# Routed experts of a mixture-of-experts encoder layer: 66 blocks of one expert with the weights standing, against 46 rounds of packed experts with the tokens standing

## The reference

```python
idx = top 6 of 64 experts per token, out of the best 4 of 8 groups
w = scores[idx] / sum * 2.5
for each expert e, for its tokens xb:
    hb = silu(xb @ w_e_gate[e]) * (xb @ w_e_up[e])      # 1024 -> 256
    routed[token] += (hb @ w_e_down[e]) * gate          # 256 -> 1024
y = layer_norm(ALPHA * x + routed + shared expert)
```

## Time and profile before

| | |
|---|---|
| runs | 2017.0, 2020.99, 2020.8 us, median 2020.8 |
| profiled execution, its own time | 2016.74 us |
| its span, first to last instruction | 2014.9 us |
| busy: PE, PEld, DVE, ACT, POOL | 95%, 65%, 32%, 17%, 11% |
| first block's first product to last block's last | 1182.48 to 1973.24 us |
| moved by DMA over the span | 337.04 MB |

### The profile page before, as it was taken

How to read it: one execution, slowest core, us unless ns; L and a number is a source line. 1 busy time by engine, 2 the same in 40 slices (tenths; PEclk the granted TensorE clock), 3 DMA queues, 4 the chain that set the end, 5 groups by cost and what they waited for, 6 DMA issues and landing times.

```text
span 2014.9 us, 24123 instructions
## 1 busy us (share of the span) xinstructions
PE 1912.1 (95%) x9388; PEld 1304.8 (65%) x9388; DVE 639.3 (32%) x1060; ACT 343.4 (17%) x453; POOL 227.0 (11%) x310
## 2 busy tenths in 40 slices
PE   6999999999999999999999989999999999999991
PEld 3444466666666555655555468887788878887781
DVE  5011158888888720012257810000000000000005
ACT  1111121111111111110013012222222222222220
POOL 0000000000000000000000412222222222222220
PEclk9999999999999999999999989999999999999996
DMA  5115011111110011111700269999999999999984
GB/s 202 42 42 188 0 42 32 32 31 31 31 31 11 11 52 52 41 43 57 283 32 22 102 212 336 330 330 337 345 333 329 327 337 329 326 329 328 336 273 146
DMA packets 129230, 337.04 MB, mean 167 GB/s; under 512 B 11664, under 2 KB 68016, under 8 KB 112304
## 3 DMA queue, kind: packets, MB, share of 16 engines
q1 hardware_dynamic: 109904, 283.13, 37.8%
q0 software_dynamic: 19296, 53.50, 12.7%
HBM read 305.65 MB, written 47.71 MB: 175 GB/s over the span
## 4 chain that ended last, share of the span: by engine, by line
PE 86%; DVE 9%; ACT 2%; issue 1%; DMA 1%; DVEq 0%; POOLq 0%; SPq 0%; ACTq 0%; POOL 0%
PE pA L873 24%; PE pg L544 10%; PE pg L571 9%; PE pg L694 8%; PE pX L884 6%; PE pB L884 6%; PE pB L725 4%; PE pB L772 2%; PE pA L772 2%; PE pA L717 2%; PE pg L584 2%; PE pB L627 2%; PE pX L785 1%; PE pA L664 1%; PE pA L627 1%
## 5 line engine op out<-in xcount | busy, mean ns | idle before, releaser
L571 PE MATMUL pg<-rA,hw 128*128 128x384 f32 x768 | 259.6, 486 | 0.7 <-ACT aTr L948 0.7
L873 PEld LDWEIGHTS pA<-rA,ew 128*128 128x128 f32 x2112 | 243.5, 194 | 16.8 <-issue 15.3
L873 PEld LDWEIGHTS pA<-rB,rEF 128*128 128x128 f32 x2112 | 241.0, 192 | 15.8 <-issue 15.8
L873 PE MATMUL pA<-rA,ew 128*128 128x128 f32 x2112 | 243.8, 277 | 1.1 <-ACT rA L1049 1.1
L873 PE MATMUL pA<-rB,rEF 128*128 128x128 f32 x2112 | 241.1, 275 | 0.0
L544 PE MATMUL pg<-rEF,rA 128*128 128x512 f32 x448 | 195.3, 598 | 3.1 <-ACT rCD L927 3.1
L571 PEld LDWEIGHTS pg<-rA,hw 128*128 128x128 f32 x768 | 140.6, 190 | 84.1 <-ACT aTr L948 0.9
L694 PE MATMUL pg<-rA,hw 128*128 128x384 f32 x512 | 165.3, 486 | 0.0
L544 PEld LDWEIGHTS pg<-rEF,rA 128*128 128x128 f32 x448 | 85.8, 192 | 110.0 <-issue 110.0
L694 PEld LDWEIGHTS pg<-rA,hw 128*128 128x128 f32 x512 | 97.2, 190 | 67.6
L1484 DVE TENSOR_TENSOR rA<-rA,pA 128x256 f32<-128x256 f32 x33 | 13.9, 422 | 387.1 <-ACT rA L1055 387.1
(11 more groups left out here) (233 smaller groups left out, 2005.3 us busy)
## 6 DMA issues: line engine op xcount, KB each, us to landing
ew<-w_e_gate SPq DMA_DIRECT2D x33, 1024.0 KB
ew<-w_e_up SPq DMA_DIRECT2D x33, 1024.0 KB
ew<-w_e_down SPq DMA_DIRECT2D x33, 1024.0 KB, 9.1
rEF<-w_e_gate SPq DMA_DIRECT2D x33, 1024.0 KB
rEF<-w_e_up SPq DMA_DIRECT2D x33, 1024.0 KB
rEF<-w_e_down SPq DMA_DIRECT2D x33, 1024.0 KB, 10.2
hw<-w_in SPq DMA_DIRECT2D x40, 512.0 KB, 3.9
rEF<-w_in SPq DMA_DIRECT2D x5, 2048.0 KB, 9.1
```

The source lines that it names most:

```text
L571: last = mm(pg[:, n * 512:n * 512 + HALF], hw3[m][:, c, :], x1T[:, c, n * HALF:(n + 1) * HALF], start=(c == 0), stop=(c == KC - 1))
L873: last = mm(pA[:, o:o + P], w[:, c, j * P:(j + 1) * P], xT[n][:, c, :], start=(c == 0), stop=(c == KC - 1))
```

## The change

**Units and rounds.** An expert's tokens get units of 32 slots instead of blocks of 128. Experts are ranked by count; a rank has a fixed number of units (`rooms`: rank 0 one, ranks 1 to 10 four, ranks 11 to 42 three, ranks 43 to 63 two; 179 in all), and the ranks come in a fixed order (`ranks_in_turn`). Four units make a round of 128 slots, so there are 45 rounds, written out one by one. What does not fit (of the expert of rank 0, 124 tokens for this input) goes into a further block of 128 in a loop: 46 rounds.

**The tokens stand.** In a round PE's `up` puts the transposed tokens of one expert in 32, 64 or 128 columns of the array and moves that expert's gate and up weights, 512 columns, past them. `pieces(t)` lists these parts: one expert's slots from an even unit on make a piece of 64, a whole round of 128, and what is left over 32. Of the 45 rounds 3 have one piece (128), 18 have two (17 times 64 and 64, once 64 and 32), 20 have three (64, 32 and 32, in one order or the other) and 4 have four of 32: 115 pieces. For each of the 8 slices of the contraction the pieces come one after the other. The down products are cut likewise. The hidden values now come out with tokens as rows and are transposed (`hidden_turn`, 2 transposes).

**Weights.** Six buffers instead of two; each of the 64 experts is loaded once, and once more the one in the rest loop, 65 loads for 66. SP can start the first after the out projection.

**A row for each slot.** `y_dram` has 8 rows for each token; the k-th expert of a token writes row k. The scatter is a plain write of the filled slots alone and does not wait for the one before. At the end 6 rows a token are loaded (18.9 MB in 12 transfers instead of 3.1 MB in 6) and summed: four by PE (products with the identity), one pair by POOL, the rest by DVE. The shared expert's result stays in SBUF; its 7 stores are gone.

**Tables.** `slots` on DVE has 26 operations where it had 16 before the first one on all 2304 columns; two of them wait for short products on PE (`ranks`, `rooms_given`).

```diff
+KSTRIDE = 8
+UNIT = 32
+UNITS = P // UNIT
+def rooms():
+    return [1] + [4] * 10 + [3] * 32 + [2] * 21
+def ranks_in_turn():
+    large, middle, small = list(range(10, 0, -1)), list(range(11, 43)), list(range(63, 42, -1))
+    first, small = small[:4], small[4:]
+    mixed = sorted(((i + 0.5) / len(g), r) for g in (large, small, middle) for i, r in enumerate(g))
+    return first + [r for _, r in mixed] + [0]
...
+def pieces(t):
+    out = []
+    for j in range(E):
+        a = max(STARTS[j], t * UNITS) - t * UNITS
+        z = min(STARTS[j + 1], (t + 1) * UNITS) - t * UNITS
+        while a < z:
+            n = 4 if a == 0 and z == 4 else 2 if a % 2 == 0 and z - a >= 2 else 1
+            out.append((j, a * UNIT, n * UNIT))
+            a += n
+    return out
...
+        weights = (rA[:, :], ew[:, :], rEF[:, EW:], rCD[:, EW:], rCD[:, 0:EW], rB[:, :])
+        gate_up = [w[:, 0:4 * D] for w in weights]
+        wd = [slabs(w[:, 4 * D:6 * D], 2) for w in weights]
...
+            sp.wait_ge(of_filled, NT)
+            for j in range(NB):
+                if j == 1:
+                    sp.wait_ge(oh_ready, 1)
+                if j == 2:
+                    sp.wait_ge(sh_gu, NT)
+                if j == 4:
+                    sp.wait_ge(oh_used, NK)
+                if j == 5:
+                    sp.wait_ge(sh_acc, NT)
+                    sp.wait_ge(x2_stored, 16 * NT)
+                e = expert_in_turn(j)
+                load_gate_up(e, j)
+                load_down(e, j)
...
+            for t in range(NR):
+                for j in range(E - NB):
+                    if last_round(j) == t:
+                        sp.wait_ge(gu_filled, t + 1)
+                        load_gate_up(expert_in_turn(j + NB), j % NB)
+                for j in range(E - NB):
+                    if last_round(j) == t - 1:
+                        sp.wait_ge(y_filled, t)
+                        load_down(expert_in_turn(j + NB), j % NB)
...
+                sp.wait_ge(rest_free, r + 1)
+                load_gate_up(e, more)
+                load_down(e, more)
...
+            yb = d["y_dram"].rearrange("(t k) n -> t k n", k=KSTRIDE)
+            for i in range(NT):
+                if i == NB - 1:
+                    sp.wait_ge(sum_filled, 1)
+                    sp.wait_ge(half_added, 1)
+                    sp.wait_ge(yb_used, 1)
+                n = i % (NB - 1)
+                for m in range(2):
+                    three = slice(3 * m, 3 * m + 3)
+                    sp.dma_start(land[n][:, three, :], yb[i * P:(i + 1) * P, three, :]).then_inc(s_yb[n][m], 16)
...
-            def up(b, n, r):
-                pe.wait_ge(xt_ready, b + 1)
-                pe.wait_ge(s_wgu[n], r * 32 + 32)
-                for m, w in ((0, wg[n]), (1, wu[n])):
-                    for j in range(2):
-                        o = n * 512 + (2 * m + j) * P
-                        for c in range(KC):
-                            last = mm(pA[:, o:o + P], w[:, c, j * P:(j + 1) * P], xT[n][:, c, :],
-                                      start=(c == 0), stop=(c == KC - 1))
+            def up(t):
+                n = t % 2
+                pe.wait_ge(xt_ready, t + 1)
+                if t >= 2:
+                    pe.wait_ge(h_ready, t - 1)
+                for j, _, _ in pieces(t):
+                    pe.wait_ge(s_wgu[j % NB], 32 * (j // NB + 1))
+                for c in range(KC):
+                    for j, o, w in pieces(t):
+                        last = mm(gu[n][o:o + w, :], xT[n][:, c, o:o + w],
+                                  at(gate_up_home(j % NB)[0], gate_up_home(j % NB)[1] + c * F, [[2 * D, 2], [1, F]]),
+                                  start=(c == 0), stop=(c == KC - 1))
...
-                    for j in range(2):
-                        last = mm(pairY[n][:, m * 512:(m + 1) * 512], hT[n][:, j, :],
-                                  wd[n][:, j, m * 512:(m + 1) * 512], start=(j == 0), stop=(j == 1))
+                    for k in range(2):
+                        for j, o, w in pieces(t):
+                            last = mm(pB[o:o + w, m * 512:(m + 1) * 512], hT[n][:, k, o:o + w],
+                                      wd[j % NB][:, k, m * 512:(m + 1) * 512], start=(k == 0), stop=(k == 1))
...
+            gathered_turn(0)
+            gathered_turn(1)
+            for t in range(NR):
+                up(t)
+                if t >= 1:
+                    down(t - 1)
+                hidden_turn(t)
+                if t + 2 <= NR:
+                    gathered_turn(t + 2)
+            down(NR - 1)
...
+                for k in range(TOPK - 2):
+                    if k == 3:
+                        pe.wait_ge(s_yb[n][1], 16 * (i // (NB - 1) + 1))
+                    for m in range(2):
+                        last = mm(pairY[i % 2][:, m * 512:(m + 1) * 512], ident,
+                                  land[n][:, k, m * 512:(m + 1) * 512], start=(k == 0), stop=(k == TOPK - 3))
...
+                ve.wait_ge(half_added, i + 1)
+                v.tensor_tensor(acc[:, i, :], acc[:, i, :], land[i % (NB - 1)][:, TOPK - 2, :], ALU.add).then_inc(yb_used, 1)
+                ve.wait_ge(yb_used, i + 1)
+                ve.wait_ge(sum_filled, i + 1)
+                v.tensor_tensor(acc[:, i, :], acc[:, i, :], pairY[i % 2][:, :], ALU.add).then_inc(sum_taken, 1)
...
+            for t in range(4):
+                gather(t)
+            for t in range(NR):
+                if t >= 1:
+                    scatter(t - 1)
+                if t + 4 <= NR:
+                    gather(t + 4)
+            scatter(NR - 1)
...
+                g.tensor_tensor(land[n][:, TOPK - 2, :], land[n][:, TOPK - 2, :], land[n][:, TOPK - 1, :],
+                                ALU.add).then_inc(half_added, 1)
```

More of the change, by code:

```diff
@@ L228, in build @@
         gate, low, high = (scratch(NK, "hw") for _ in range(3))
-        nblk, incl, base = (scratch(E, "hw") for _ in range(3))
+        starts_rep, rooms_rep = scratch(P, "hw"), scratch(P, "hw")
+        keyrow, ahead, match, given, over = (work[:, n * E:(n + 1) * E] for n in range(5))
+        base, room = given, work[:, 5 * E:6 * E]
+        rest, resti_n, incl, shift = (work[:, n * E:(n + 1) * E] for n in range(6, 10))
+        keycol = second[:, 0:1]
+        beyond = work[:, 10 * E:(10 + NT) * E]
         OH = P + 2 * NCOL
-        OH_FLIGHT = KC * D // OH
+        OH_FLIGHT = EW // OH
         def oh_place(x):
@@ L267, in build @@
         pairY = [pB, pX]
+        gu = [pA[:, n * 512:(n + 1) * 512] for n in range(2)]
+        hTp = [slabs(pX[:, n * 512:n * 512 + F], 2) for n in range(2)]
         def logits_at(i):
@@ new lines, in hidden_turn, with down @@
+            def hidden_turn(t):
+                n = t % 2
+                pe.wait_ge(h_ready, t + 1)
+                if t >= 2:
+                    pe.wait_ge(ht_ready, t - 1)
+                for k in range(2):
+                    last = tr(hTp[n][:, k, :], hid[n][:, k * P:(k + 1) * P], ident)
+                    if k == 0 and t == last_round(more + NB * (used - 1)) + 1:
+                        last.then_inc(rest_free, 1)
+                last.then_inc(ht_filled, 1)
+            def down(t):
+                n = t % 2
+                pe.wait_ge(ht_ready, t + 1)
+                if t >= 1:
+                    pe.wait_ge(y_ready, t)
+                for j, _, _ in pieces(t):
+                    pe.wait_ge(s_wd[j % NB], 16 * (j // NB + 1))
@@ new lines, in weighted @@
+            def weighted(t):
+                n = t % 2
+                sc.wait_ge(y_filled, t + 1)
+                if t >= 2:
+                    sc.wait_ge(y_stored[n], 16 * (t // 2))
+                fn(yrow[n], pB[:, :], ACT.Copy, scale=tblg[:, t:t + 1]).then_inc(y_ready, 1)
+            gathered(0)
+            gathered(1)
+            for t in range(NR):
+                silu(t)
+                if t >= 1:
+                    weighted(t - 1)
+                hidden_turned(t)
+                if t + 2 <= NR:
+                    gathered(t + 2)
@@ L1487, in gate_column @@
-            def gate_column(b, n, first=False):
-                if not first:
-                    ve.wait_ge(y_ready, b - 1)
-                v.tensor_copy(gcol[n], tblg[:, bass.ds(b, 1)]).then_inc(gc_ready, 1)
-            for n in range(2):
-                hidden(n, n, True)
-                gate_column(n, n, True)
-            with ve.Fori(1, pairs) as r:
-                for n in range(2):
-                    hidden(r * 2 + n, n)
-                    gate_column(r * 2 + n, n)
-            ve.wait_ge(s_ln2, 32)
@@ L1572, in _, with gather @@
-            scatter(last_block, 1, chain, pairs)
-            for n in range(2):
-                po.wait_ge(xg_loaded[n], pairs * 16 + 16)
+            nrest = po.value_load(nbi[0:1, 0:1], min_val=1, max_val=NREST)
+            def gather(t):
+                if t >= 2:
+                    po.wait_ge(xt_filled, t - 1)
```

(2 more changed lines are left out.)

459 lines of the change are left out of this document (278 added, 181 removed).

## The result

The changed kernel takes **2086.5 us** (2085.1 to 2087.3, four runs), the kernel before beside it 2020.5 (2017.0 to 2021.0): a ratio of 1.033, 95% interval 1.0312 to 1.0348. It is 3.3% slower; the forecast was 3% faster.

The account below looks back on a forecast made before the run. PE was taken to bound the routed experts, with DMA just keeping up. From 2016.7 us, -91 for the rounds, +4 for slots and +26 for the tail gave 1956, or 1960 on the median's scale; range 1840 to 2260.

Parts of the forecast that it names:

- The bound before, and room on the DMA engines: Routed experts: PE sets the pace and DMA just keeps up; after the change transfers need 582 us, under PE's 700.
- The 582 us for all transfers: Routed experts' DMA work after the change: 472 us of weight loads plus 110 of gathers and scatters, range 563 to 680.
- Then a slice of p pieces takes p times 0.43 us, or 0.86 if p is 1.: PE's products in the rounds: records start in program order, so rounds take 12.0, 17.2 or 22.3 us; stage -91 us.
- rival 1: Rounds: column groups overlap fully, every round 12.0 us on PE, so transfers become the bound; 1850 us, chance 0.18.
- rival 2: Mixed rounds: changing between widths 64 and 32 drains the array, preventing overlap; 2252 us, or 2107; chance 0.22 in all.
- Changes of the standing width, some two at 0.15 us: PE's side cost per round, within 1.7 us that also holds ten transposes (1.1 us) and joints (0.3).
- the in-order premise: PE's rounds: a piece's first record can start with the previous piece's second record, but not earlier; 0.43 us a piece.
- Rival 2, in its form with full overlap inside a width: Mixed rounds: width changes drain the array, equal widths overlap fully; 2.02 us a slice, stage 847, time 2107, chance 0.08.
- Rivals 3 and 4: PE's rounds: standing loads show, 0.57 us a piece, 2148 us, chance 0.10; or no overlap at all, 2538 us, 0.08.
- Slots, +4: Before the rounds: the longer `slots` chain on DVE takes about 8 us instead of 4.0, delaying PE's next shared-expert products.
- The tail, +26: Behind the rounds: loading and summing 18.9 MB of slot rows makes 68 us from the last product instead of 41.7.
- my own case: Whole kernel: pieces overlap partly, in program order, giving 1960 us, 3% faster; own range 1915 to 2010, chance 0.40.

## Why the prediction was wrong, point by point

- **The bound before, and room on the DMA engines.** Right. PE without waits for weights, a share of 0.75 for a forecast of about 0.8. Gathers and scatters take 4.5% of 2085.0 us, 94 us, where I took 110 and had 95 as the lower end. The 582 us for all transfers agree with the kernel of 32s everywhere, whose stage takes 580 us (1194.10 to 1774.2), but in part by luck: where the DMA engines were full they moved 409 to 416 GB/s, more than I had taken, and the first 40 and last 60 us, with shares of 0.90 and 0.59, used up the difference.
- **"Then a slice of p pieces takes p times 0.43 us, or 0.86 if p is 1."** Wrong for every round of more than one piece. Pieces of one width start together and cost 0.86 for any number: rounds of two 64s took 11.7 us, for a forecast 12.0 that came out near for a wrong reason, and those of four 32s 11.85, where 22.3 were forecast. I held the order of issue to be the order of streaming. The trace shows four records starting within 0.02 us. This error alone would have made the forecast too slow, not too fast: rival 1 had the opposite premise, that each column group takes its records on its own, and within one width it held. The Trainium skill has it in the same place as the rule of rival 2 ("TensorEngine Tiling (Array Packing)", Key Properties): tiles operate independently and can load and multiply in parallel. The trace agrees.
- **"Changes of the standing width, some two at 0.15 us" a round.** This is the step that failed and turned the sign. It counted the changes from and to 128, and gave 64 to 32 to a rival with 0.22. A round that mixes widths in both products has 25 changes (24 with a seam), each 0.13 us, and what counts more, nothing overlaps across one. Its price was taken rightly from the earlier trace rows (0.15 a change). Its place was wrong: a slice of 64, 32, 32 that I had at 1.29 us takes 1.99, and rounds that I had at 17 us take up to 25. Had the in-order premise been put right and this one not, the forecast would have been the 1850 of rival 1.
- **Rival 2, in its form with full overlap inside a width.** This happened: 2.02 us a slice and 847 us for the stage, 2107 in all, were forecast with 0.08; measured are 1.99, 819.5 and 2086.5. Of the 28 us between the two stages, transposes and joints of 1.24 to 1.4 us a round instead of 1.7 make 19, slices of 1.985 for 2.02 make 9, the six seams 6 and the cold start 1 (1.4 for 2.7). Some 7 go the other way: the rest block takes 14.6 for 12.0, and there are PE's waits and the 2 us that the count leaves open. "It decides once a slice of three costs over 1.9 us" stands beside a slice of 1.99. The Trainium skill's rule that changing the tiling mode drains TensorE named the mechanism outright; I held against it that 64 and 32 both leave the other half of the columns alone. The trace decides for the rule: a change between 64 and 32 keeps the two from overlapping whether the 64 stands in the first or in the second half of the columns.
- **Rivals 3 and 4.** Out: no 0.57 between pieces, no rounds of two 64s at 22 us. The price of no overlap is real where columns are shared (the four ups sent to the same columns, +85 us).
- **Slots, +4.** Measured +4.4 for the chain, but +11.8 for the start of the stage. The term missed three things. The chain begins 1.5 us later. The gathered rows come 3.2 us later after their gather, with two experts' loads beside it; no run takes the loads away, so that they are the cause isn't shown. And a second block of transposes stands ahead of the first `up` (+2.0), which the diff shows and I did not cost.
- **The tail, +26.** Measured +29.6: 71.3 us for a forecast of 68. The loads began 5.8 us behind the last product for a forecast 8.3, they took 49 us for 47, and what follows the last one took 16.4 for 13; some 1.4 of it is DVE's operation beside POOL's addition.
- **The range** held the time since it reached to the rivals of the other side; my own case's range, 1915 to 2010, did not.

## What to carry to other kernels

When narrow products are packed beside each other in the array, let everything between two changes have one width, even if a piece must be cut in two: two 32s of one expert cost no more than a 64 (rounds of 11.69 and 11.71 us), while a 64 between 32s costs its whole length and two changes. When a sum rests on which operations overlap, list each neighbouring pair in issue order by its shape, and count the pairs that differ; here the premise counted two changes a round where there were up to 25. And when one side of a tuned pair gets fast, the other is next at once: here the transfers stood 39 us behind PE.

## What the runs showed of the hardware

- **Overlap reaches across lines of code.** At the seam of `up` and `down`, the 32s of the last slice of `up` and those of the first slice of `down` load and run together, four in all; PEld's timeline of the changed kernel:

```profile
1337.02 0.11 PEld L1020 LDWEIGHTS pA<-rB,aTr 128*32 128x32 f32 x1 [0.81 <-issue]
...
1337.03 0.11 PEld L1046 LDWEIGHTS pB<-rCD,rows 128*32 128x32 f32 x2
...
1338.01 0.19 PEld L1046 LDWEIGHTS pB<-rCD,rows 128*64 128x64 f32 x2 [0.84 <-issue]
```

  The six mixed rounds with such a seam take 24.1 us, the three without 25.06: half a slice is saved.
- **A fused operation of DVE stands still beside POOL's addition.** Five of six L1333 in the changed kernel, which reads two tiles in SBUF, ended 1.07 to 1.08 us after POOL's addition; the statistics at 2051.55, which read one, kept their 1.42 us for two with POOL's addition from 2051.58 to 2053.93 beside them. The Trainium skill ("SBUF — State Buffer", Who interferes with whom) says that a DVE instruction with two inputs in SBUF contends with a GpSimd instruction that reads SBUF, and that one with at most one such input doesn't, outside some faster modes. The trace agrees with both.
- **The granted clock fell in the stage in which PE waited for weights.** In the kernel with 32s everywhere it is 1.00 where PE is busy 160.0 of 160 us and 0.96 where it is busy 292.9 of 320. After a wait of 7.24 us for weights, for one, the records from 1435.01 on come 0.83 us apart instead of 0.43, at a granted clock of 0.50 (1431.3 to 1437.9). With fewer bytes to wait for it is 1.00 in every window from 1234 us to the last product. So a stage held by its transfers pays a little on PE too.
- **Transfers went at 409 to 416 GB/s** in the windows above in which loads, gathers and scatters ran together at a DMA share of 1.01 to 1.02, more than the 396 of the earlier trace rows. Gathers and plain scatters moved 37.8 MB in 94 us of the 16 engines' time, 402 GB/s, where gathers and scatters with an addition went at 209. How much of that is the addition itself isn't shown: the change also writes fewer rows and to other places.
